# Two attentions of a fused transformer kernel, worked through in pairs of heads

## The reference, cut to what matters

```
q_full = concat(q_nope[128], q_pe[64]); k_full = concat(k_nope[128], k_pe[64], shared by the heads)
o_mla  = causal_attention(q_full, k_full, v_mla)            # MLA: 8 heads, 256 queries, 256 keys
y      = gates[0]*o_mla + gates[1]*o_gla + gates[2]*o_mem;  x = x + y @ w_o
```

```
o_a = windowed_attention(q_a, k_a, v_a, k_ctx, v_ctx, sink)   # |i-j| <= 128, softmax with a sink
o_b = softmax(q_b @ [k_b, k_b_ctx].T / 8) @ [v_b, v_b_ctx]
x   = layer_norm(ALPHA*x + gate1 * ((g_a*(o_a @ w_a) + g_b*(o_b @ w_b)) @ w_out)); ...
```

## Time and profile before

| | |
|---|---|
| time of three runs, median (lowest to highest) | 1012.34 us (1011.33 to 1013.93) |
| the profiled execution: its own time, its span | 1012.67 us, 1011.1 us |
| mean granted TensorE clock, share of full | 0.985 |
| TensorE matmul busy | 961.3 us (95%), 4652 matmuls |
| TensorE weight load busy | 766.0 us (76%) |
| VectorE, ScalarE, GpSimd busy | 747.0 (74%), 551.7 (55%), 168.2 (17%) us |
| DMA | 175.11 MB, mean 173 GB/s |
| chain that ended last | PE 75%, DVE 13%, ACT 6%, issue 5%, DMA 2% |

### The profile page before, as it was taken

The page is one execution under the profiler, slowest core; times in us unless marked ns, Lnnn a source line. Parts: engine busy times, 40 slices in busy tenths (PEclk is TensorE's granted clock), DMA queues, the critical chain, the costliest instruction groups (busy, mean ns, idle before and its releaser), DMA issues.

```text
span 1011.1 us, 13813 instructions
## 1 busy us (share of the span) xinstructions
PE 961.3 (95%) x4652; PEld 766.0 (76%) x4652; DVE 747.0 (74%) x1086; ACT 551.7 (55%) x816; POOL 168.2 (17%) x250
## 2 busy tenths in 40 slices
PE   7999999998999899999999999999999699999995
PEld 6787887876767778888888887777777588777884
DVE  5787467876676778886778796756567979999945
ACT  6557646465765455555333436755543367777532
POOL 7000000118100000110111011530000313333400
PEclk9999999998999999999999999999999899999998
DMA  8675443865542347886789564211225255556551
GB/s 259 208 249 156 140 157 123 299 199 172 167 156 88 132 135 243 268 265 213 251 293 316 179 208 148 74 63 50 76 82 189 63 180 168 171 169 215 177 188 41
DMA packets 99746, 175.11 MB, mean 173 GB/s; under 512 B 8252, under 2 KB 36444, under 8 KB 99692
## 3 DMA queue, kind: packets, MB, share of 16 engines
q1 hardware_dynamic: 92460, 148.87, 45.5%
q0 software_dynamic: 7184, 25.50, 7.5%
q10 hardware_dynamic: 48, 0.04, 0.0%
HBM read 173.33 MB, written 1.05 MB: 172 GB/s over the span
## 4 chain that ended last, share of the span: by engine, by line
PE 75%; DVE 13%; ACT 6%; issue 5%; DMA 2%; DVEq 0%; SPq 0%; ACTq 0%
PE acc L706 58%; DVE wlo L1650 3%; PE scores L1108 3%; PE turned L1116 3%; PE turned L758 2%; ACT whi L1233 2%; DVE ltb_lo L1690 1%; DMA raw<-in_w_mem_kv 1%; PE turned L732 1%; DVE turn L1705 1%; PE scores L969 1%; PE scores L902 1%; DVE conv L2385 1%; PE scores L968 1%; DVE turn L1708 1%
## 5 line engine op out<-in xcount | busy, mean ns | idle before, releaser
L1650 DVE TENSOR_TENSOR wlo<-raw,whi 128x1024 fp32r<-128x1024 f32 (+2 forms) x270 | 346.3, 1304 | 111.6 <-ACT whi L1233 103.0
L1233 ACT CAST whi<-raw 128x1024 fp32r<-128x1024 f32 (+2 forms) x270 | 273.5, 1030 | 193.0 <-PE acc L706 148.7
L706 PE MATMUL acc<-whi,lta_lo 128*128 128x512 f32 (+2 forms) x576 | 228.4, 397 | 4.9 <-DVE lta_lo L1690 3.3
L706 PE MATMUL acc<-wlo,lta_hi 128*128 128x512 f32 (+2 forms) x576 | 222.8, 387 | 0.0
L706 PE MATMUL acc<-whi,lta_hi 128*128 128x512 f32 (+2 forms) x576 | 222.5, 386 | 0.0
L706 PEld LDWEIGHTS acc<-whi,lta_lo 128*128 128x128 f32 x576 | 108.6, 189 | 39.5 <-issue 13.5
L706 PEld LDWEIGHTS acc<-wlo,lta_hi 128*128 128x128 f32 x576 | 108.5, 188 | 22.1
L706 PEld LDWEIGHTS acc<-whi,lta_hi 128*128 128x128 f32 x576 | 108.7, 189 | 19.7
L706 PE MATMUL acc<-whi,ltb_lo 128*128 128x512 f32 (+1 forms) x272 | 110.3, 406 | 7.9 <-DVE ltb_lo L1690 4.1
L602 POOL DMA_DIRECT2D wm<-in_w_mod x48 | 34.4, 719 | 466.4 <-DVEq L1750 268.4
L706 PE MATMUL acc<-whi,ltb_hi 128*128 128x512 f32 (+1 forms) x272 | 107.2, 394 | 0.0
(11 more groups left out here) (341 smaller groups left out, 1414.7 us busy)
## 6 DMA issues: line engine op xcount, KB each, us to landing
raw<-in_w_in SPq DMA_DIRECT2D x88, 512.0 KB, 4.1
wm<-in_w_mod POOLq DMA_DIRECT2D x48, 512.0 KB, 5.6
raw<-in_w_up SPq DMA_DIRECT2D x88, 256.0 KB, 3.0
raw<-in_w_up SPq DMA_DIRECT2D x32, 512.0 KB, 4.5
raw<-in_w_down SPq DMA_DIRECT2D x32, 512.0 KB, 4.9
raw<-in_w_down SPq DMA_DIRECT2D x44, 256.0 KB, 3.3
raw<-in_w_mem_kv SPq DMA_DIRECT2D x8, 512.0 KB, 5.8
raw<-in_w_o SPq DMA_DIRECT2D x8, 512.0 KB, 3.4
```

The source lines that it names most:

```text
L706: ins = pe.matmul(acc[s][:, t, 0:n], lhs[part][:, kt0 + kk, tok], w[:, u % RING, kk, 0:n], start=(k == 0 and kk == 0 and j == 0), stop=(la ...
L1233: act.copy(whi[:, s, :, 0:n], raw[:, s, :, 0:n]).then_inc(hi_ready, 1)
L1650: dve.tensor_tensor(wlo[:, s, :, 0:n], raw[:, s, :, 0:n], whi[:, s, :, 0:n].bitcast(F32), ALU.subtract)\
```

## The change

Heads (MLA) or heads of the same key head (AB) are taken in pairs p: 4 in MLA, 16 in AB. A new `attend_pairs` on each of the three engines takes the place of `attend` for both. The two 64-row score products of a pair lie in the two halves of the partitions, go to the two banks of sc, and are issued back to back. In MLA, for each query block, the two 128-row products come first, then the two 64-row products. TensorE's order in a pair is: both turns of pair p, scores of pair p+1, values of pair p, weight units, extra work. The value products of a pair go to one bank of tb. Two units per pair are done in MLA, 14 units over 15 pairs in AB. The places of the extra work get new numbers. All six sums of squares (`norm_sums`) are done after pair 0. In the excerpt `exp(p)` and `softmax(p)` do both heads of a pair, each head behind its own semaphore.

```
-AB_KEYS, AB_QUERIES, AB_OUT = 12, 13, 18
-AB_GATE = 2
+AB_KEYS, AB_QUERIES, AB_OUT = 5, 6, 8
+AB_GATE = 1
+def mla_units(p):
+    return 2 * p
+def ab_units(p):
+    n, steps = (3 * KT + 2 * KT // 2) // UNIT - AB_LAST, AB_PAIRS - 1
+    return min(n, (2 * n * p + 3 * steps) // (2 * steps)) if p > 0 else 0
+IN_DONE, BA_DONE = [ab_done(4 * c) + 1 for c in (1, 2, 3)], AB_PAIRS - 1
...
 TensorE
+            def attend_pairs(name, n, scores, blocks, values, fill_units, after=None):
+                def score(p):
+                    banks = [s_begin(f"{name}.{2 * p + e}") for e in range(2)]
+                    for ins, (_, full) in zip(scores(p, [bank for bank, _ in banks]), banks):
+                        ins.then_inc(full, 1)
+                score(0)
+                for p in range(n):
+                    for e in range(2):
+                        i = 2 * p + e
+                        b, k = S_USE[f"{name}.{i}"]
+                        pe.wait_ge(s_free[b], k + 2)
+                        bank, full = t_begin(f"{name}.PT{i}")
+                        for j in range(blocks):
+                            ins = pe.transpose(bank[:, P * j:P * j + P], prob[:, e, P * j:P * j + P], ident[:])
+                        ins.then_inc(full, 1)
+                    if p + 1 < n:
+                        score(p + 1)
+                    for e in range(2):
+                        b, k = T_USE[f"{name}.PT{2 * p + e}"]
+                        pe.wait_ge(t_free[b], k + 2)
+                    bank, full = t_begin(f"{name}.O{p}")
+                    values(p, bank).then_inc(full, 1)
+                    fill_units(p)
+                    if after:
+                        after(p)
...
+            def mla_scores(p, banks):
+                last = [None, None]
                 for t in range(T):
+                    for e in range(2):
+                        pe.matmul(banks[e][:, P * t:P * t + P * (t + 1)], qnT[:, 2 * p + e, P * t:P * t + P],
+                                  knT[:, 2 * p + e, 0:P * (t + 1)], start=True, stop=False)
+                    for e in range(2):
+                        lane = slice(64 * e, 64 * e + 64)
+                        last[e] = pe.matmul(banks[e][:, P * t:P * t + P * (t + 1)], qrT[lane, p, P * t:P * t + P],
+                                            kpT[lane, 0:P * (t + 1)], start=False, stop=True)
+                return last
...
+            def ab_scores(p, banks):
+                br, hp, t = ab_pair(p)
+                if p == AB_PAIRS // 2:
+                    turned("kB.0", "kB.1", "qB.0", "qB.1")
+                return [pe.matmul(banks[e][:, :], qT[br][64 * e:64 * e + 64, hp, P * t:P * t + P],
+                                  kT[br][64 * e:64 * e + 64, 2 * hp // GROUP, :], start=True, stop=True)
+                        for e in range(2)]
...
 ScalarE
+            def attend_pairs(name, n, exps, first, units, blocks, after=None):
+                ahead(first)
+                exp(0)
+                for p in range(n):
+                    if p >= 1:
+                        b, k = T_USE[f"{name}.O{p - 1}"]
+                        act.wait_ge(t_full[b], k + 1)
+                    for e in range(2):
+                        t_out(f"{name}.PT{2 * p + e}", probT[:, e, 0:P * blocks], P * blocks)
+                    ahead(first + units(p))
+                    if p + 1 < n:
+                        exp(p + 1)
+                        ahead(first + units(p + 1))
+                    if after:
+                        after(p)
...
-                if i in (0, 3, 7):
-                    gate(("G11", "G00", "G01")[(i + 1) // 4])
+                if p in (0, 1, 3):
+                    gate(("G11", "G00", "G01")[(p + 1) // 2])
...
 VectorE
+            def attend_pairs(name, n, maxima, sums, weigh, first, units, after=None):
+                ahead(first)
+                softmax(0)
+                for p in range(n):
+                    ahead(first + units(p))
+                    if p + 1 < n:
+                        softmax(p + 1)
+                    for e in range(2):
+                        b, k = S_USE[f"{name}.{2 * p + e}"]
+                        dve.wait_ge(s_free[b], k + 2)
+                        sums(2 * p + e, rows_of(p)[e])
+                    b, k = T_USE[f"{name}.O{p}"]
+                    dve.wait_ge(t_full[b], k + 1)
+                    for e in range(2):
+                        ins = weigh(2 * p + e, e, rows_of(p)[e][:, 8:10], tb[b])
+                    ins.then_inc(t_free[b], 1)
+                    ahead(first + units(p + 1))
+                    if after:
+                        after(p)
...
+            def mla_after(p):
+                if p == 1:
                     gate_on("G11", r_gla)
                     done(dve.tensor_tensor(r_gla, r_gla, o_mem, ALU.add))
+                elif p == 2:
                     mix(0)
+                if p in (0, 1, 3):
+                    gate_in_psum(("G11", "G00", "G01")[(p + 1) // 2])
...
+                if i == 0:
+                    for t in range(T):
+                        dve.wait_ge(ev("ab_sq"), t + 1)
+                        norm_sums(t)
+                    var(stat[:, 2:4, :], HD).then_inc(ev("ab_var"), 1)
+                elif i == 1:
                     inverse("ab", stat[:, 2:4, :])
```

More of the change, by code:

```diff
@@ L141 @@
 MOD_TURN = (9, 14, 22, 27)
-AB_STEPS = 2 * HEADS * T
+MLA_PAIRS, AB_PAIRS = H_MLA // 2, HEADS * T
 AB_FILL = ["IN4", "IN5", "IN6", "BA0", "BA1"]
 AB_LAST = 2
-def ab_units(i):
-    n, steps = (3 * KT + 2 * KT // 2) // UNIT - AB_LAST, AB_STEPS - 1
-    return min(n, (2 * n * i + 3 * steps) // (2 * steps)) if i > 0 else 0
+def mla_units(p):
[3 more added lines that the diff above has]
+    return min(n, (2 * n * p + 3 * steps) // (2 * steps)) if p > 0 else 0
 def ab_done(units):
-    return next(i for i in range(AB_STEPS) if ab_units(i + 1) >= units)
-IN_DONE, BA_DONE = [ab_done(4 * c) for c in (1, 2, 3)], ab_done(14)
+    return next(p for p in range(AB_PAIRS) if ab_units(p + 1) >= units)
+IN_DONE, BA_DONE = [ab_done(4 * c) + 1 for c in (1, 2, 3)], AB_PAIRS - 1
 def t_names():
@@ L171, in t_names @@
     out += ["qn.0", "qn.1", "qn.2", "qn.3", "qr.0", "qr.1", "kp"] + g("kn", 4)
-    out += attention_t("MLA", H_MLA)
+    out += pairs_t("MLA", MLA_PAIRS)
     out += g("y", 4) + g("hc", 4) + g("h2", 4)
@@ new lines, in mla_scores, with mla_values @@
+                    for e in range(2):
[3 more added lines that the diff above has]
+                return last
+            def mla_values(p, bank):
+                for e in range(2):
+                    h = 2 * p + e
+                    for t in range(T):
+                        for kt in range(t + 1):
+                            ins = pe.matmul(bank[:, 256 * e + P * t:256 * e + P * t + P],
+                                            probT[:, e, P * (t + kt):P * (t + kt) + P],
+                                            kv[:, kt, 256 * h + P:256 * h + 2 * P], start=(kt == 0), stop=(kt == t))
+                return ins
@@ L983, in _, with mla_fill @@
+            def mla_fill(p):
+                for j in range(mla_units(p), mla_units(p + 1)):
+                    unit(f"G0{j // 4}", j % 4, lta)
+            attend_pairs("MLA", MLA_PAIRS, mla_scores, 3, mla_values, mla_fill)
             turn_tokens("y", r_gla, ready="branches_mixed", groups=(0, 1))
@@ L1127, in ab_unit, with ab_fill @@
                 unit(AB_FILL[3 + (j - 12) // 2], j % 2, ltb, first_kt=2 * (j % 2))
-            def ab_fill(i):
-                for j in range(ab_units(i), ab_units(i + 1)):
+            def ab_fill(p):
+                for j in range(ab_units(p), ab_units(p + 1)):
                     ab_unit(j)
```

123 lines of the change are left out of this document (54 added, 69 removed).

## The result

The changed kernel takes 1022.77 us (median of 4 runs, 1018.28 to 1026.15), the kernel before in the same comparison 1012.16 us: a ratio of 1.0095, 95% interval 1.0072 to 1.0118. It is 1% slower. The forecast was 1015.9 us within 1002 to 1027, with 0.46 for slower. The sign and the range held, and the cost was about three times what was forecast: +10.4 us against the median of 1012.34, instead of +3.6.

A forecast was written before the change was run, and what follows sets the result against it. The prediction took TensorE's order and occupancy to bound both attentions, with the softmax hidden. Overlap -24.6, waits +24.0 and clock +4.2 gave +3.6 us: 1016.3 for the profiled execution, 1015.9 for the median, range 1002 to 1027.

The forecast's parts named there:

- Term 1: Score products of a pair overlap fully on TensorE, saving 19.2 us in AB and 5.4 in MLA, 24.6 together.
- rivals 2 and 3: Score products: strict issue order gives half the overlap, 1021.5 us, chance 0.12; or halves run one after the other, 1027.4, 0.13.
- rival 2: Score products in AB and MLA: strict order of issue gives only half of the overlap, 1021.5 us; chance 0.12.
- Term 2: Software pipeline in AB and MLA loses its distance, so TensorE waits 24.0 us more; bounds 10 and 30.
- three AB waits of 2 us or more: TensorE idle before value products in AB's pairs 3, 7 and 12, released by ScalarE's copy: 2.6, 2.1 and 2.0 us.
- Rival 1: Free time of VectorE and ScalarE mostly covers the waits for copies in both attentions: faster, 1005 us; chance 0.33.
- nothing can cover the two starts: Said against the faster case: idle time at the starts, 3.6 us in MLA and 3.5 + 0.5 in AB, cannot be covered.
- Term 3: TensorE's clock drops after idle time at both starts and MLA's pair 1: three losses of 1.4, 4.2 us; bounds 0 and 7.

The follow-up runs named there:

- third experiment: Changed kernel with both 64-row score products of a pair reading the same partition half: 1030.3 us, ratio 1.0185 to the kernel before.
- tenth experiment: Changed kernel with AB's sigmoids and square root behind copies, a bias add earlier in MLA, one weight unit ahead of each attention's first turns: 1002.2 us.
- Experiment 5: Changed kernel with AB's gate sigmoids behind the next pair's copies and MLA pair 1's bias add ahead of the gate product and addition: 1010.9 us.
- Experiment 11: Kernel before the change, with each AB gate sigmoid moved behind the next step's copy on ScalarE: 1012.5 us, ratio 1.0010.
- experiment 10: Changed kernel with AB's sigmoids and square root behind copies, a bias add earlier in MLA, one weight unit ahead of each attention's first turns: ratio 0.9884.
- fourth experiment: Changed kernel with spare matmuls in TensorE's idle time at the starts of MLA and AB: 1017.8 us, ratio 1.0057 to the kernel before.
- second experiment: Pairs in AB alone, MLA as in the kernel before: 1018.4 us, ratio 1.0054 to the kernel before.
- after: The changed kernel as it stands, pairs in both MLA and AB, against the kernel before: 1022.8 us, ratio 1.0095.

## Why the prediction held in sign and missed in size

**Term 1, the overlap, was right in kind and 3 us too large.** Full overlap: 1.06 us for four matmuls (rivals 2 and 3 asked for 1.6 and 2.0), shown by the third experiment. The pair period was forecast as 7.8 - 1.2 = 6.6 and is 6.67. Over the whole of AB the busy time fell by 15.6 us, not 19.2. The scores alone give 17.6 (busy 35.62 us before, 18.06 in the tenth experiment). About 2 us come back, by an estimate from the rows, because TensorE stands 15 times in the tenth experiment's AB and twice in that of before: the matmul ahead of such a stop is busy for its full 0.27 us, where the next otherwise starts 0.11 after it, 13 x 0.16 = 2.1. In MLA 6.0 came for 5.4; a pair's scores take 2.66 us for 2.62. The Trainium skill, "TensorE: Matmul & The Clock Gate", Part 3, says that row groups run together, which the trace bears out, and that matmuls start and end in strict program order. Worked out as in rival 2, that order allowed half of this gain; the 1.06 us decide against it. So do the single starts: the second product's first matmul starts at 658.78, 0.53 us ahead of the first product's second. With both products in one half the second and the fourth matmul report a product, as issued, and in two halves the third and the fourth.

**Term 2, the waits, was right in its places and 4 us too large.** Forecast and measured, in us: start of AB 3.5 + 0.5 and 3.20, pair 0 1.5 and 1.87, pairs 1, 5 and 6 together 1.0 and 0.95, pair 3 2.6 and 2.45, pair 7 0.6 + 2.1 and 0.58 + 1.46, pair 8 0.8 and 0.51, pair 12 2.0 and 1.29, last 1.2 and 0.96; MLA's start 3.6 and 3.22, its pair 0 0.35 and none, pair 1 3.55 and 3.45, pair 2 0.85 and 0.74. Together TensorE's idle time grew by 19.9 for 24.0. Of the three AB waits of 2 us or more that the prediction named as its sign, only that of pair 3 is so long; 1.46 and 1.29 are under it, so the blocks behind pairs 7 and 12 were timed too late. AB without its clock term was forecast as 125.3 - 19.2 + 15.8 = 121.9 and is 108.7 + 13.3 = 122.0: both terms were 3.6 too large and cancelled, which is luck. MLA up to WO0 without its clock term was forecast as 53.9 and is 42.58 + 10.16 = 52.7. Experiment 5 shows the cause that was named: moving the sigmoids and one bias add out of the way of the copies is worth 10 to 12 us with pairs. Experiment 11 shows that the sigmoids' part is worth nothing without them. The bias add's part is not shown to come from the pairs as such, since the change also moved the addition into its block.

**Rival 1 was wrong where the prediction said so:** the free 30 to 40% of ScalarE and VectorE did not cover the waits, because the copies stood behind other work in the queue. Its remark that nothing can cover the two starts was wrong: in experiment 10 a weight unit leaves 0.50 us there in MLA, and 0.27 and 0.20 in AB.

**Term 3, the clock, is the step that failed.** It was 4.2 us with bounds of 0 and 7, and it is 13.8. Both factors were too low: six stretches at 2.3 us each, for three at 1.4. The number of losses: three places with 3.5 us or more of idle time were counted. The granted clock fell at the two starts and in MLA's pair 1, as said, and also around the values of AB's pairs 1, 8 and 13, with single waits of 1.87, 1.46 and 1.29 us (0.58 more comes 3 us ahead of the second). After the 2.45 us before pair 4's values it did not fall. And the price: 1.4 us was read from a unit that lay only partly in such a stretch. At the start of AB the clock stays at 1.2 GHz for 10 us of nearly full work, and the fourth experiment prices this place at 3.95 us. The 13.8 us themselves are a difference of busy times of two kernels, so their last microsecond is uncertain.

The Trainium skill, "TensorE: Matmul & The Clock Gate", Part 1 (on the oscillation of the clock), puts the extra time at half of the time spent at the lower clock. For AB the mean granted clock gives an estimate of 0.09 x 131.3 = 11.8 us by that rule, and the busy times give 9.3. The rule comes out high here. TensorE is idle in part of the slow stretches (busy 7.81 us from 697 to 706, at a mean clock of 0.62), which is the likely reason.

Sum of the misses: overlap +3.0, waits -4.1, clock +9.6, outside the attentions -3.0, together +5.5, which is 9.1 less 3.6.

## What to carry to other kernels

A software pipeline made of pairs saves work on the bound engine, but here it took a step of slack from every copy: look at what stands ahead of the copy in the helper's queue (a sigmoid, a square root, a bias add from a third engine) and move it behind in the same change. Price the idle time that comes in on TensorE twice, once as a wait and once as the pace of what follows, and use a real unit of work to fill it only when the later waits are gone. Cancelling terms look alike in a median; the busy, idle and clock columns of one stretch tell them apart.

## What was unexpected of the hardware

Two 64-row f32 products of 512 columns in different partition halves, two matmuls each, take 1.06 us together, in one half 1.91. Added matmuls made the kernel faster by 4 to 5 us, because the ones behind them ran at 2.4 instead of 1.2 GHz. And the clock varies between executions of the same instructions: with AB's waits about the same (13.7 and 13.3 us of idle time), AB's busy time was 121.0 us in the second experiment and 118.0 in after. Around pair 4's values the clock stayed at 1.00 in after (665 to 677 us, a wait of 2.45) and fell to a mean of 0.72 in the fourth experiment (660 to 672 us, a wait of 2.31). What decides it between two executions these runs do not show.
